# Hybrid encoder layer: where a modulation quarter's sums stand among the scan's mask products, and the attention projection written out with two accumulators

## What is computed

```python
ada = jnp.dot(jax.nn.silu(c), w_ada) + b_ada
shift1, scale1, gate1, shift2, scale2, gate2 = jnp.split(ada[:, None, :], 6, axis=-1)
h = layer_norm(x) * (1 + scale1) + shift1
z, xbc, dt_raw, q_a, kv_a, k_r, g_logits = jnp.split(jnp.dot(h, w_in), IN_OFFSETS, axis=-1)
y_ssd = ssd_branch(z, xbc, dt_raw, conv_w, conv_b, dt_bias, A_log, D_skip, ssd_norm_w, w_ssd_out)
y_mla = mla_branch(q_a, kv_a, k_r, cos, sin, q_norm_w, w_uq, kv_norm_w, w_ukv, w_mla_out)
g = jax.nn.sigmoid((g_logits + b_gate).astype(jnp.float32)).astype(x.dtype).reshape(b, s, N_BRANCH, d)
mix = jnp.dot(g[:, :, 0] * y_ssd + g[:, :, 1] * y_mla, w_mix_out)
x = post_layer_norm(DEEPNORM_ALPHA * x + (1 + gate1) * mix, ln1_g, ln1_b)
h2 = layer_norm(x) * (1 + scale2) + shift2
f = peer_ffn(h2, peer_w_q, peer_keys_1, peer_keys_2, peer_u, peer_v)
```

## Time and profile before

| | us |
|---|---|
| median of three runs | 2928.09 |
| lowest and highest run | 2924.17, 2930.9 |
| the profiled execution | 2929.89 |
| its span, first to last instruction | 2928.2 |
| attention projection, TensorE's first to last unit | about 423.5 to 534 |
| scan, 8 groups | about 534 to 1114 |

### The profile page before, as it was taken

The page is one execution under the profiler, slowest core; times in us unless marked ns, Lnnn a source line. Parts: engine busy times, 40 slices in busy tenths (PEclk is TensorE's granted clock), DMA queues, the critical chain, the costliest instruction groups (busy, mean ns, idle before and its releaser), DMA issues.

```text
span 2928.2 us, 37718 instructions
## 1 busy us (share of the span) xinstructions
PE 2319.1 (79%) x13830; PEld 1941.1 (66%) x13830; DVE 2166.9 (74%) x2578; ACT 949.3 (32%) x1305; POOL 895.2 (31%) x725
## 2 busy tenths in 40 slices
PE   4689998999999999999869645444454569999990
PEld 3589998988888889999659645444454454444440
DVE  7757678788878785444565889889998896666568
ACT  1144442344444444433343212215656630000000
POOL 0000001222222220000100576675665815444343
PEclk9699999999999999999989877776666679999995
DMA  8655658655555554655533899998989929999995
GB/s 341 288 178 202 223 201 300 235 206 204 208 201 202 197 204 173 222 184 186 209 144 137 345 384 371 391 364 356 383 359 375 406 91 408 414 414 414 414 409 228
DMA packets 144949, 817.68 MB, mean 279 GB/s; under 512 B 16520, under 2 KB 21248, under 8 KB 70832
## 3 DMA queue, kind: packets, MB, share of 16 engines
q0 software_dynamic: 93200, 477.21, 41.8%
q1 hardware_dynamic: 49728, 336.05, 30.7%
q10 hardware_dynamic: 1888, 2.59, 0.2%
HBM read 811.55 MB, written 4.23 MB: 279 GB/s over the span
## 4 chain that ended last, share of the span: by engine, by line
PE 39%; DVE 25%; DMA 21%; issue 9%; ACT 3%; POOL 2%; DVEq 1%; ACTq 0%; POOLq 0%
DMA vrow<-in_p_vg,acc 12%; PE ps L654 9%; PE ps L656 9%; PE ps L655 9%; DMA rrow<-in_peer_u,acc 6%; DVE rrow L2019 6%; DVE ps L2056 3%; DVE wlo L1465 2%; ACT whi L1059 2%; DVE acc L1514 2%; PE ps L634 2%; PE ps L636 2%; PE ps L635 2%; POOL rrow L2191 1%; DVE oh L2069 1%
## 5 line engine op out<-in xcount | busy, mean ns | idle before, releaser
L1465 DVE TENSOR_TENSOR wlo<-raw,whi 128x2048 fp32r<-128x2048 f32 x216 | 513.6, 2380 | 372.4 <-ACT whi L1059 363.0
L1059 ACT ACTIVATE whi<-raw 128x2048 fp32r<-128x2048 f32 x216 | 412.7, 1913 | 705.0 <-PE ps L656 480.5
L2191 POOL DMA_INDIRECT rrow<-in_peer_u,acc x256 | 459.2, 1794 | 452.9 <-DVE acc L1964 202.3
L2019 DVE CUSTOM_DVE_ANT_0 rrow<-rrow,h 128x2048 f32<-128x2048 f32 x216 | 485.5, 2289 | 27.8 <-DMA rrow<-in_peer_u,acc 26.0
L654 PE MATMUL ps<-h_hi,whi 128*128 128x256 f32 (+1 forms) x1568 | 453.9, 289 | 9.6 <-issue 5.0
L2056 DVE SCALAR_TENSOR_TENSOR ps<-vrow,acc,ps 128x1024 f32<-128x1024 f32 x254 | 327.2, 1288 | 163.7 <-DMA vrow<-in_p_vg,acc 145.2
L655 PE MATMUL ps<-h_lo,whi 128*128 128x256 f32 (+1 forms) x1568 | 444.0, 283 | 0.0
L656 PE MATMUL ps<-h_hi,wlo 128*128 128x256 f32 (+1 forms) x1568 | 443.9, 283 | 0.0
L2191 POOL DMA_INDIRECT vrow<-in_p_vg,acc x256 | 248.8, 972 | 320.4 <-DVE ps L2056 232.2
L654 PEld LDWEIGHTS ps<-h_hi,whi 128*128 128x128 f32 (+1 forms) x1568 | 299.6, 191 | 22.7 <-issue 15.0
L994 PE MATMUL ps<-con,rrow 128*128 128x128 f32 x640 | 133.3, 395 | 228.6 <-DMA rrow<-in_peer_u,acc 227.8
(11 more groups left out here) (337 smaller groups left out, 4441.9 us busy)
## 6 DMA issues: line engine op xcount, KB each, us to landing
raw<-in_p_in SPq DMA_DIRECT2D x104, 1024.0 KB, 5.0
ada_in<-in_p_ada POOLq DMA_DIRECT2D x128, 512.0 KB
vden<-in_p_vd SPq DMA_DIRECT2D x64, 1024.0 KB
ada_in<-in_p_ada SPq DMA_DIRECT2D x32, 1024.0 KB, 9.3
raw<-in_p_so SPq DMA_DIRECT2D x32, 1024.0 KB, 4.8
raw<-in_p_mo SPq DMA_DIRECT2D x16, 1024.0 KB, 6.8
raw<-in_p_bc SPq DMA_DIRECT2D x16, 1024.0 KB, 4.8
raw<-in_p_mix SPq DMA_DIRECT2D x16, 1024.0 KB, 4.8
```

Source lines behind the costliest of these rows:

```text
L1059: F(whi[:, n % 2, :, 0:cols_], raw[:, n % 4, :, 0:cols_], ACT.Copy).then_inc(hi_ready, 1)
L1465: V.tensor_tensor(wlo[:, n % 2, :, 0:cols_], raw[:, n % 4, :, 0:cols_], whi[:, n % 2, :, 0:cols_].bitcast(F32), ALU.subtract).then_inc(lo_ ...
L2019: last = V.tensor_tensor_reduce(row, row, h2[:, b, :], 1.0, 0.0, ALU.mult, ALU.add, dots[:, k, e:e + 1])
L2191: return G.indirect_dma_start(out=dst, out_offset=None, in_=table, in_offset=bass.IndirectOffsetOnAxis(ap=eid_all[:, r:r + 1], axis=0))
```

## The change

In the scan, quarter 2 of the modulation moves on VectorE from ahead of `lo(9)` to behind the four mask products. In the attention projection the loops on TensorE, ScalarE and VectorE are written out (SyncE's and GpSimd's stay). Slab s accumulates in `acc[:, s % 2]`, so its first quarter waits only for the sum before the last. TensorE does the sum of slab s - 1 behind the first unit of slab s, VectorE adds its bias behind the first `lo` of slab s, and ScalarE stores it behind the second `hi` of slab s, directly ahead of fetching the next bias. The last slab's sum, row and store stay at the end.

```diff
-                with pe.Fori(0, 2) as i:
-
-                    pe.wait_ge(row_ready, i * 2 + (ADA_MLA + 1))
-                    for s in range(2):
-                        for q in range(4):
-
-                            pe.wait_ge(o_split, q + 1)
-                            channel_unit(U_MLA, 4 * s + q, i, N_MLA, oT_hi, oT_lo, 4 * q, DC - 1, slab_tiles(1 - s))
-                        if s:
-                            pe.wait_ge(row_ready, i * 2 + (ADA_MLA + 2))
-                        sum_slab(aux[:, 0, :], 0, i * 2 + (ADA_MLA + s))
+                pe.wait_ge(row_ready, ADA_MLA + 1)
+                for s in range(4):
+                    for q in range(4):
+
+                        pe.wait_ge(o_split, q + 1)
+                        channel_unit(U_MLA, 4 * s + q, 0, 0, oT_hi, oT_lo, 4 * q, DC - 1, slab_tiles(1 - s % 2))
+                        if s and q == 0:
+                            if s > 1:
+                                pe.wait_ge(row_ready, ADA_MLA + s)
+                            sum_slab(aux[:, 0, :], (s - 1) % 2, ADA_MLA + s - 1)
+                pe.wait_ge(row_ready, ADA_MLA + 4)
+                sum_slab(aux[:, 0, :], 1, ADA_MLA + 3)
...
-                with act.Fori(0, 2) as i:
-                    for s in range(2):
-                        for q in range(4):
-                            hi(U_MLA, 4 * s + q + 2, i, N_MLA)
-                            if q == 1:
-                                ada2_bias(i * 2 + (ADA_MLA + s))
-                        ada2_store(i * 2 + (ADA_MLA + s))
+                for s in range(4):
+                    for q in range(4):
+                        hi(U_MLA, 4 * s + q + 2, 0, 0)
+                        if q == 1:
+                            if s:
+                                ada2_store(ADA_MLA + s - 1)
+                            ada2_bias(ADA_MLA + s)
+                ada2_store(ADA_MLA + 3)
...
+                    two = not in_ssd and isinstance(slab, int) and slab > ADA_MLA
+                    dve.wait_ge(acc_summed, slab + (QUARTERS + 2) - (1 if two else 0))
...
+                for s in range(4):
+                    for q in range(4):
+                        ada2(ADA_MLA + s, q, into=s % 2)
+                        lo(U_MLA, 4 * s + q + 2, 0, 0)
+                        if s and q == 0:
+                            ada2_row(aux[:, 0, :], ADA_MLA + s - 1)
+                    slab_done(U_MLA, 4 * s + 3, 0, 0)
...
                         lo(U_SSD, u + 8, i, N_SSD)
-                        ada2(slab, 2, True)
                         lo(U_SSD, u + 9, i, N_SSD)
...
                             V.tensor_tensor(m, m, cbm[:, k // 2, :].unsqueeze(1).broadcast_to([P, 4, P]), ALU.mult)\
                                 .then_inc(mt_ready, 1)
+                        ada2(slab, 2, True)
                         lo(U_SSD, u + 10, i, N_SSD)
                         ada2(slab, 3, True)
                         lo(U_SSD, u + 11, i, N_SSD)
```

More of the change, by code:

```diff
@@ L1598, in _, with ada2 @@
                 S.step(last) if k == 0 else last.then_inc(angles_ready, 1)
-            def ada2(slab, q, in_ssd=False):
+            def ada2(slab, q, in_ssd=False, into=0):
                 if q == 0:
-                    dve.wait_ge(acc_summed, slab + (QUARTERS + 2))
+                    two = not in_ssd and isinstance(slab, int) and slab > ADA_MLA
+                    dve.wait_ge(acc_summed, slab + (QUARTERS + 2) - (1 if two else 0))
                 for e in range(2):
@@ L1610, in ada2 @@
                         dve.wait_ge(ada2_full[j % 4], slab * 32 + 16 * (j // 4 + 1))
-                    last = ada_rows_in(acc[:, 0, :], ada2_in[:, 2 + e if in_ssd else j % 4], 4 * q + 2 * e, 2)
+                    last = ada_rows_in(acc[:, into, :], ada2_in[:, 2 + e if in_ssd else j % 4], 4 * q + 2 * e, 2)
                     if j == 7:
@@ L1743, in _ @@
                 dve.wait_ge(b_free, 5)
-                with dve.Fori(0, 2) as i:
-                    S.enter(i, 4 + 2 * (DC - 1))
-                    for s in range(2):
-                        slab = i * 2 + (ADA_MLA + s)
-                        for q in range(4):
-                            ada2(slab, q)
-                            lo(U_MLA, 4 * s + q + 2, i, N_MLA)
-                        slab_done(U_MLA, 4 * s + 3, i, N_MLA)
-                        for k in range(2):
-                            m = premix[:, ds(i * 8 + (4 * s + 2 * k), 2), :]
-                            S.step(V.tensor_tensor(m, ps[:, 1 - s, k, :].rearrange("p (k t) -> p k t", t=SEQ), m,
-                                                   ALU.mult))
-                        ada2_row(aux[:, 0, :], slab)
-                S.leave(2)
+                for s in range(4):
[5 more added lines that the diff above has]
+                    slab_done(U_MLA, 4 * s + 3, 0, 0)
+                    for k in range(2):
+                        m = premix[:, 4 * s + 2 * k:4 * s + 2 * k + 2, :]
+                        S.step(V.tensor_tensor(m, ps[:, 1 - s % 2, k, :].rearrange("p (k t) -> p k t", t=SEQ), m,
+                                               ALU.mult))
+                ada2_row(aux[:, 0, :], ADA_MLA + 3)
             if on("ssd"):
```

## The result

| | before | after |
|---|---|---|
| median of 14 runs each, side by side, us | 2928.80 (2923.38 to 2932.80) | 2935.57 (2932.34 to 2937.46) |
| ratio, 95% interval | | 1.0025 [1.0018, 1.0032] |
| profiled execution: time, span | 2929.89, 2928.2 | 2932.34, 2930.6 |

The change makes the kernel slower by a quarter of a percent. The forecast was 2925, and its range held the time. The profiled execution of after is the lowest of its 14. So the profiles differ by 2.4 us and the medians by 6.8, and the profile shows the loss smaller than it is.

What follows compares the result with a forecast made beforehand. TensorE was taken to set the pace, with each scan group a race of VectorE's and TensorE's roads to unit 12. 2928.2 - 11.3 + 8 gave 2926.6; with the median 1.8 lower, the forecast was 2925 us, range 2910 to 2939.

Steps and rivals of the forecast that it cites:

- Part 1, the projection: Attention projection: each slab end costs TensorE only the sum, 0.95 us; gains 1.97, 7.32 and 1.98, together 11.3 us.
- Rival 4: Attention projection doesn't give its 11 us, since the store's landing or the loads hold it up: 2936 us; chance 0.05.
- The masks: Scan, VectorE: masks end 9.6 us after t, the start of hi(9), range 8.7 to 11.3, where they ended at 11.3.
- Quarter 3's load: Scan: first load issued only once quarter 2's first tile is free, landing in 4.2 us, range 3.5 to 6.3.
- the end at t + 19.4: Scan, VectorE: quarter 3 waits 1.0 us for its load and ends 19.4 us after hi(9) starts, not 16.7.
- VectorE's road: Scan: VectorE reaches the end of lo(12) 14.1 us after quarter 3's end, allowing unit 12 at t + 33.5.
- TensorE's road: Scan: TensorE waits for the sum from t + 16.4 to 19.5, then reaches unit 12 at t + 32.0, 34.8 with jump.
- term of 1.5: Scan: TensorE's clock falls behind the new wait half of the time, costing 1.6 us in two loop groups: + 1.5 us.
- The two loop groups: Scan, groups with TensorE's loop jump: the fourth changes by - 0.6 us, the sixth by + 0.9.
- already hidden: Scan, four groups: the 2.3 us gap and slow unit 9 were partly hidden by VectorE's road; removing them returns nothing.
- The scan's part: Scan: + 6.5 us over the eight groups and + 1.5 for TensorE's clock, + 8 us in all.
- rival 2: Scan: quarter 3 ends after t + 20.6, through late masks (2938 us) or a slower load (2933 to 2941); chance 0.22.

Runs made afterwards that it cites:

- e9: The changed kernel with seven unused 128 x 128 products on TensorE ahead of the scan's sum; 2926.8 us, ratio 0.9993 to the kernel before.
- e10: e7 with five unused 128 x 128 products on TensorE ahead of unit 9; 2897.8 us, ratio 0.9894 to the kernel before.
- e7: e1 with TensorE's loop over the scan written out; 2910.4 us, ratio 0.9943 to the kernel before.
- e8: e3 with TensorE's loop over the scan written out; 2911.6 us, ratio 0.9949 to the kernel before.
- e12: e9 with TensorE's loop over the scan written out; 2924.6 us, ratio 0.9991 to the kernel before.
- e3: The changed kernel with a third 512 KB tile for the scan's modulation, letting quarter 3's first load go out early; 2921.3 us, ratio 0.9982 to the kernel before.
- e1: The changed kernel with the scan's old order put back, so the projection's part alone; 2914.6 us, ratio 0.9958 to the kernel before.
- e2: The kernel before with only quarter 2's move in the scan; 2946.4 us, ratio 1.0064 to the kernel before.
- e6: e1 with a third tile for the scan's modulation; 2918.7 us, ratio 0.9969 to the kernel before.
- e5: The changed kernel with quarter 2 between lo(9) and the mask products; 2922.8 us, ratio 0.9983 to the kernel before.

## Why the prediction was wrong

- **Part 1, the projection**: right in mechanism and nearly in size, 10.5 for 11.3 us. `hi` at 5.76 and 6.89 us, no low clock at 480, store and bias hidden. Rival 4 didn't happen.
- **The masks**: forecast t + 9.6, measured 8.4 to 8.9. `lo(9)` waited for the end of `xend` as said, but `xend` ended at t + 2.6 (721.73) instead of 3.3. That quarter 2 no longer stood beside GpSimd's products is the likely reason, not tested by itself. The step left out this consequence of the move.
- **Quarter 3's load**: forecast 4.2 us from issue to landing. The first tile took 4.1 to 5.3, the second 4.9 to 5.6. The load's share of the lateness was estimated too low and the masks' too high. The two errors cancel, so that the end at t + 19.4 came out right by luck. Taking the landing from the pair's mean rate gave a lower end, not a middle. The waits of the earlier trace rows were nearer.
- **VectorE's road**, + 14.1 from quarter 3's end, t + 33.5 for the end of `lo(12)`: measured t + 33.0 to 33.9 in six groups. Right. In the two with a jump it is 36.5 and 36.6, since `hi(12)` waits there for TensorE's late unit 10.
- **TensorE's road: the step that failed.** The working had TensorE wait from t + 16.4 to 19.5 and then go on at full speed, to unit 12 at t + 32.0, or 34.8 with the jump. For the clock it put down 1.5 us in all, because "half of the time" the clock falls and it costs something in the two loop groups only. In fact it fell in eight groups of eight. TensorE reached unit 12 at t + 34.8 and 34.6 in the third and the last group, 0.9 and 1.3 us after `lo(12)` was there, and at t + 37.8 and 37.9 in the loop groups, 3.0 and 3.1 us later than forecast. In the third group (rows above) sum and start of unit 10 are 1.79 us apart where 0.95 was forecast, and units 10 and 11 take 13.1 us where 11.5 was. Together that is some 8 us, so the term of 1.5 is mis-sized by some 7 us. Filling the wait gives back 8.8 us by the medians (e9), though not visibly in these groups of its trace. The wait itself was nearly right, idle for 3.1 to 3.9 us where 3.1 was put down.
- **The two loop groups** were to gain 0.6 and lose 0.9; they lost 2.4 and 3.0. Slow sum, jump and slow unit 10 add up on TensorE there. The jump itself took 2.57 and 2.59 us of idle time, a little less than the 2.76 of the row at 823.65, but in other kernels it takes 1.0 to 4.8. The sixth group was also misread. Its t + 33.5 is the end of `lo(12)`, while in the kernel before TensorE, slow behind the jump, reached unit 12 only at 982.30 = t + 34.8:

```profile
982.30 0.28 PE L654 MATMUL ps<-h_hi,whi 128*128 128x256 f32 x1
```

By the working's own 34.8 that group was to stay level. With the 33.5 that it used, the difference is 1.3 and not 0.9.
- **The reading of the kernel before** had a flaw that bears on all this. The four groups whose unit 12 waits for `wlo` were read as groups in which VectorE's road decides and hides the slow unit 9. e10 shows the contrary. With the clock held they take 70.1 to 70.8 us like the others, because `wlo` itself had been late from TensorE's slow unit 9: a group with a slow unit 9 is 2.3 us longer (72.80 against 70.47 in e7). The road named by the releaser was not independent of the other. That the old gap's cost was "already hidden" was therefore wrong, and 12 us could be had without moving anything: 12.5 by the medians of e7 and e10, and five such groups of 2.3 us in the trace of the kernel before.
- **The execution**: the sum was made against one profile, and the profile of after was the lowest of its runs. The scan's part is + 13.6 there and about + 17 by the medians (6.8 + 10.5). What its other runs had more of can't be read, since only one has a trace.

Of the rivals, rival 2 gave the outcome (2935.6 lies in its 2933 to 2941), but not by its own point: it decided from quarter 3's end after t + 20.6, and no group of after came to that. Its time was right by luck.

## What to carry to other kernels

Before a step is moved, follow its buffers: here the load that could go out only behind the moved step set the end of the whole group, and a third tile, or moving the step half as far, took about two thirds of the loss away. When TensorE waits a few microseconds, price the wait and the clock behind it separately, in the old order as well as in the new, and follow the slow unit to the buffers it holds; a releaser named at the end of that chain may itself have been held by it. If TensorE must wait anyway, a handful of unused products in the gap can be worth more than removing the gap: e10, which keeps its gap and fills it, is 13.8 us faster than e8, which has removed it. And before a difference of medians is explained by a mechanism, look in the traces whether it lies in the stage that was changed.

## What the runs showed of the hardware that was not expected

- **Unused products pay**: five products per group, 2.3 us each time, took 12.5 us off the kernel (e7 to e10) with unit 9 starting as late as it did. Behind waits of 2.2 to 2.7 us (start to start, e7 and before) the granted clock fell in some groups and not in others of the same run; behind 3.7 to 4.5 us (after) it fell every time, to 0.5 for 3.4 us and more. In e12 it stayed at 1.00 through waits of up to 2.2 us from start to start ahead of unit 12, and in e10, where no two products from 526 to 1112 us start more than 0.6 us apart, it stayed at 1.00 too.
- **A loop's jump on TensorE has no fixed price.** The idle time of the kernel before is 2.76 us. At the same jump behind the fourth group it is 2.57 in after (row above), 3.68 in e9, 4.82 in e3, and in e1 and e2:

```profile
808.96 0.38 PE L654 MATMUL ps<-h_hi,whi 128*128 128x256 f32 x1 [1.01 <-issue]
```

```profile
828.85 0.57 PE L654 MATMUL ps<-h_hi,whi 128*128 128x256 f32 x1 [4.00 <-issue]
```

During e3's, the DMA queue for instructions moves one packet beside the data queues (window 804 to 813, queue, packets, MB, share of the engines):

```profile
q1 hardware_dynamic: 238, 1.81, 53.7%
q0 software_dynamic: 289, 1.05, 36.0%
q8 instruction: 1, 0.02, 0.7%
```

The packet has 16 KB. In the nine kernels that keep the loop TensorE resumes 1.5 to 1.7 us after the end of such a packet, at each of the 17 jumps that leave it idle for over 0.9 us. The packet starts from 1.6 us before TensorE stands still (e6) to 2.4 us after (e3), and the idle time goes with that. What holds the packet back was not tested. Busy data queues alone don't explain it, since e5's jump behind the fourth group has the DMA engines nearly all busy too and leaves TensorE idle for 2.41 us. The Trainium skill (Runtime: NRT & Kernel Launch, Instruction fetch mechanics) says that a branch to code not at hand waits for a DMA fetch. The rows agree with that: the idle time is 0.9 to 4.8 us here and ends behind the packet every time.
